# Gates projected with channels on the partitions, and probabilities divided by their sums

## The reference

```
h = RMSNorm(x);  P = h @ w_in[l]                 # (rows, 1024) @ (1024, columns of four branches)
A: sparse attention over the top 256 keys by an index score, 4 heads, one K/V head
B: attention with a forgetting term F[t] - F[s] on the logits, 4 heads, s <= t
C: attention in a band of 9 chunks of 64, learned bias on t - s, 4 heads
M: attention into 256 memory rows, 4 heads
parts = [o * silu(P[gate columns of the branch])  for the four outputs o]   # 256 columns each
x = x + concat(parts) @ w_out[l]
```

## Time and profile before

| what | value |
|---|---|
| median of 3 runs | 1713.21 us |
| lowest, highest | 1713.04, 1716.13 us |
| the profiled execution's own time | 1712.33 us |
| its span (first to last instruction) | 1710.5 us |
| TensorE busy | 1692.7 us, 99% |
| VectorE busy | 1005.7 us, 59% |
| ScalarE busy | 662.3 us, 39% |
| GpSimd busy | 239.7 us, 14% |
| granted TensorE clock, mean | 0.999 |

### The profile page before, as it was taken

The page is one execution under the profiler, slowest core; times in us unless marked ns, Lnnn a source line. Parts: engine busy times, 40 slices in busy tenths (PEclk is TensorE's granted clock), DMA queues, the critical chain, the costliest instruction groups (busy, mean ns, idle before and its releaser), DMA issues.

```text
span 1710.5 us, 30251 instructions
## 1 busy us (share of the span) xinstructions
PE 1692.7 (99%) x10866; PEld 1103.7 (65%) x10866; DVE 1005.7 (59%) x2707; ACT 662.3 (39%) x1599; POOL 239.7 (14%) x452
## 2 busy tenths in 40 slices
PE   9999999999999999999999999999999999999998
PEld 4466677767778755555444677767777886555553
DVE  3645888778878333333235378887888772333321
ACT  4532334333343345454124323343333433445531
POOL 1233321100010010002012433220000001000000
PEclk9999999999999999999999999999999999999999
DMA  8344322223132322114421533231231324221130
GB/s 285 94 143 126 127 94 87 97 78 106 41 134 94 103 79 97 40 47 115 129 94 51 166 104 127 94 137 44 81 109 38 132 97 121 69 90 37 46 108 37
DMA packets 60340, 166.64 MB, mean 97 GB/s; under 512 B 11345, under 2 KB 29745, under 8 KB 57889
## 3 DMA queue, kind: packets, MB, share of 16 engines
q1 hardware_dynamic: 43584, 125.88, 23.0%
q0 software_dynamic: 16608, 38.83, 6.9%
HBM read 137.03 MB, written 30.73 MB: 98 GB/s over the span
## 4 chain that ended last, share of the span: by engine, by line
PE 80%; DVE 14%; DMA 2%; issue 2%; ACT 1%; DVEq 1%; ACTq 0%; SPq 0%
PE psX L876 54%; DVE lower L1268 9%; PE psT L816 7%; PE psX L1052 6%; PE psS L985 6%; DVE work L1490 2%; PE psS L904 2%; DMA wring<-in_w 2%; PE psS L816 1%; PE psX L816 1%; PE psX L1027 1%; DVE gate L1322 0%; PE psS L954 0%; PE psS L924 0%; DVE sc L1434 0%
## 5 line engine op out<-in xcount | busy, mean ns | idle before, releaser
L876 PE MATMUL psX<-wring,hT 128*128 128x512 f32 (+2 forms) x2016 | 834.3, 557 | 6.4 <-ACT kv L1146 3.0
L876 PEld LDWEIGHTS psX<-wring,hT 128*128 128x128 f32 x2016 | 363.9, 190 | 327.5 <-issue 318.6
L1268 DVE TENSOR_SCALAR_CACHE_REDUCE lower<-sc,thr 128x640 uint8<-128x640 f32 (+5 forms) x462 | 407.3, 934 | 17.5 <-issue 9.5
L876 PE MATMUL psX<-hT,wring 128*128 128x128 f32 x2880 | 334.6, 275 | 0.9 <-ACT gate L1166 0.4
L876 PEld LDWEIGHTS psX<-hT,wring 128*128 128x128 f32 x2880 | 327.7, 192 | 3.6 <-issue 3.0
L1208 ACT ACTIVATE work<-work,stat 128x256 f32<-128x256 f32 (+7 forms) x288 | 200.0, 694 | 295.9 <-DVEq L1493 293.3
L1217 ACT COPY work<-psT 128x512 f32<-128x512 f32 (+2 forms) x352 | 156.7, 488 | 321.0 <-PE psT L816 319.7
L816 PEld LDWEIGHTS psT<-con,work 128*128 128x128 f32 x1080 | 121.4, 141 | 73.2 <-issue 66.5
L816 PE MATMUL psT<-con,work 128*128 128x128 f32 x1080 | 158.2, 278 | 0.0
L1490 DVE CUSTOM_DVE_ANT_0 work<-psS,bias 128x640 f32<-128x640 f32 (+7 forms) x120 | 86.2, 718 | 41.9 <-issue 20.5
L1490 DVE CUSTOM_DVE_ANT_0 work<-psS,sc 128x384 f32<-128x384 f32 (+5 forms) x48 | 42.8, 891 | 72.1 <-PE psT L816 70.0
(11 more groups left out here) (203 smaller groups left out, 1537.9 us busy)
## 6 DMA issues: line engine op xcount, KB each, us to landing
wring<-in_w SPq DMA_DIRECT2D x17, 2048.0 KB, 9.4
cache<-in_kB SPq DMA_DIRECT2D x16, 512.0 KB, 7.0
cache<-in_vB SPq DMA_DIRECT2D x16, 512.0 KB, 4.1
cache<-in_kC SPq DMA_DIRECT2D x16, 512.0 KB, 6.8
cache<-in_vC SPq DMA_DIRECT2D x16, 512.0 KB, 4.7
scratch_oscr<-gate POOLq DMA_DIRECT2D x54, 128.0 KB, 2.0
hT<-scratch_oscr SPq DMA_DIRECT2D x18, 384.0 KB, 3.6
kv<-in_x SPq DMA_DIRECT2D x9, 512.0 KB, 5.7
```

The costliest lines, as they stand in the source:

```text
L876: mm = pe.matmul(out, lhs, rhs, start=(kt == 0), stop=(kt == KT - 1))
L1268: v.tensor_scalar(lower[:, at:at + STRIP_L[t]], sc[:, o], thr[:, n:n + 1], 0.0, ALU.is_lt, ALU.add, accum_out=below[:, n:n + 1])
```

## The change

The gates' columns now come first in B2, C2 and A2, and two blocks of them are turned; M1 is turned whole. So the gate leaves the projection with its channels on the partitions, as the gating wants it, and V needs no transposes of it and ScalarE no copy (L1223). R is written with the two operands exchanged, so that its result comes out turned, and GT is gone.

A row's reciprocal can't be multiplied into a gate that has rows along the free axis. It is multiplied into the probabilities instead, before T: Z is split into Z 0 and the last Z. Z 0 takes the reciprocals of the even heads on VectorE, and ScalarE multiplies their exponentials (L1222 after); the other takes those of the odd heads, and VectorE multiplies them itself (L1499 after). T of a pack waits for its multiplications and not for its exponentials. Z 0 stands ahead of L 1, the last Z behind the second half of the selection's rounds, before the end of the unit. A pack's sums for samples are still divided where they were (L1513).

```diff
-TURNED = {"mm": 2, "B1": 4, "C1": 4, "M1": 2}
+TURNED = {"mm": 2, "B1": 4, "B2": 2, "C1": 4, "C2": 2, "M1": 4, "A2": 2}
@@ program_order
-        if prev:
-            emit("Z", prev)
         if prev and not fresh:
             emit("T", prev, 0)
...
             if pack and len(buffers(pack)) == 2:
+                emit("Z", pack, 0)
                 emit("L", pack, 1)
...
+    def weigh():
+        if pipe[0] and not weighed[0]:
+            emit("Z", pipe[0], buffers(pipe[0])[-1])
+            weighed[0] = True
...
     def settle():
         odd_heads()
+        weigh()
+        weighed[0] = False
...
         odd_heads()
         select(pace[0] / 2)
+        weigh()
         emit("P", c, t)
@@ TensorE, T
-                    pe.wait_ge(*probs.on((p, [i for i in range(heads(p)) if i % 2 == hp][-1])))
+                    if is_sample(p):
+                        pe.wait_ge(*probs.on((p, 0)))
+                    else:
+                        pe.wait_ge(*weighed[hp].on(p))
@@ TensorE, V
-                    pe.wait_ge(*scaled.on(p))
...
-                    for i in range(0, nh, 2):
-                        g = (h0 + i) // 2
-                        turn(o[:, W + i // 2 * P:W + (i // 2 + 1) * P], gates(br)[:, t, g * P:(g + 1) * P])
@@ TensorE, R
-                            mm = pe.matmul(X.ap(s)[32 * j:32 * j + 32, g * P:(g + 1) * P],
-                                           con[:, C_SELG + 32 * g:C_SELG + 32 * g + 32], om[:, j, :], start=True, stop=True)
+                            mm = pe.matmul(X.ap(s)[:, g * P + 32 * j:g * P + 32 * j + 32], om[:, j, :],
+                                           con[:, C_SELG + 32 * g:C_SELG + 32 * g + 32], start=True, stop=True)
@@ ScalarE, after a unit
+                        xg, rest = (x[:, W:2 * W], None) if c == "M1" else (x[:, 0:W], x[:, W:2 * W])
@@ ScalarE
-                elif k == "V" and not is_sample(s[1]):
-                    br, t, h0, nh = s[1]
-                    act.wait_ge(*X.fill(s).on(s))
-                    nc.scalar.copy(merged(br, t, h0 // 2, nh // 2),
-                                   X.ap(s)[:, W:W + nh * HD].rearrange("p (g c) -> p g c", g=nh // 2))
-                    act.drain().then_inc(g_turned.sem, 1)
+                elif k == "Z" and s[2] == 0 and not is_sample(s[1]):
+                    p = s[1]
+                    act.wait_ge(*inverted.on(p))
+                    for i in range(0, heads(p), 2):
+                        x = buf(0)[:, offset(p, i):offset(p, i) + blocks(p) * P]
+                        last = nc.scalar.mul(x, x, stats(p)[:, 2, i:i + 1])
+                    last.then_inc(weighed[0].sem, 1)
@@ VectorE, Z
-                    dve.wait_ge(*probs.on((p, n - 1)))
-                    v.reciprocal(stats(p)[:, 2, 0:n], stats(p)[:, 1, 0:n])
+                    dve.wait_ge(*probs.on((p, [i for i in range(n) if i % 2 == hp][-1])))
+                    last = v.reciprocal(stats(p)[:, 2, hp:n:2], stats(p)[:, 1, hp:n:2])
+                    if hp == 0 and not is_sample(p):
+                        last.then_inc(inverted.sem, 1)
                     dve.drain()
-                    if not is_sample(p):
-                        ga = gates(br)[:, t, h0 * HD:(h0 + n) * HD].rearrange("p (h d) -> p h d", h=n)
-                        v.tensor_tensor(ga, ga, stats(p)[:, 2, 0:n].unsqueeze(2).to_broadcast([P, n, HD]), ALU.mult)
-                        dve.drain()
-                    dve.drain().then_inc(scaled.sem, 1)
+                    if hp:
+                        for i in range(1, n, 2):
+                            x = buf(hp)[:, offset(p, i):offset(p, i) + blocks(p) * P]
+                            last = v.tensor_scalar(x, x, stats(p)[:, 2, i:i + 1], None, ALU.mult)
+                        last.then_inc(weighed[1].sem, 1)
@@ the weights' columns
-... "B2": join("b_v", "b_g") ... "C2": join("c_v", "c_g") ... "A2": join("a_q", "a_g")
+... "B2": join("b_g", "b_v") ... "C2": join("c_g", "c_v") ... "A2": join("a_g", "a_q")
```

More of the change, by code:

```diff
@@ L207, in settle @@
             emit("R", old[0])
-            gather.append(old[0])
     def project(c, t):
@@ L319, in program_order @@
         to_norm, normed = [], []
-        while queue or pipe != [None, None] or gather or outs or to_norm:
-            work = bool(queue) or pipe != [None, None] or bool(gather)
+        while queue or pipe != [None, None] or outs or to_norm:
+            work = bool(queue) or pipe != [None, None]
             if work:
@@ L331, in program_order @@
                     normed.append(t)
-            done = [s for s in o if s[0] == l and s[1][0] in ("V", "GT")]
-            ready = lambda t: (l, ("GT", "A")) in done if t == ST_ else (l, ("V", packs_of("A", t)[-1])) in done
+            done = [s for s in o if s[0] == l and s[1][0] in ("V", "R")]
+            ready = lambda t: (l, ("R", "A")) in done if t == ST_ else (l, ("V", packs_of("A", t)[-1])) in done
             if outs and ready(outs[0][1]):
@@ L650, in encoder @@
         pt_act = Signal(sem("probs_turned"), packs)
-        scaled = Signal(sem("gate_scaled"), packs)
-        g_turned = Signal(sem("gate_turned"), [p for p in packs if not is_sample(p[1])])
+        prompts = [p for p in packs if not is_sample(p[1])]
+        inverted = Signal(sem("sums_inverted"), prompts)
+        weighed = [Signal(sem(f"probs{hp}_weighed"), prompts) for hp in range(2)]
         om_ready = Signal(sem("own_heads_kept"), [p for p in packs if is_sample(p[1])])
         gated = Signal(sem("branch_gated"), [(l, s[1]) for l, s in order if s[0] == "R" or (s[0] == "V" and not is_sample(s[1]))])
-        gathered = Signal(sem("samples_turned"), events(["GT"], lambda s: s[1]))
         selected = Signal(sem("selected"), [(l, s[1][1]) for l, s in order if s[0] == "K" and s[1][0] == "mask"])
@@ L1067, in _ @@
                     turn(T.ap(s)[:, 0:P], om[:, 2, :]).then_inc(T.fill(s).sem, 1)
-                elif k == "GT":
-                    br = s[1]
-                    pe.wait_ge(*gated.on(br))
-                    pe.wait_ge(T.empty(s).sem, T.free(s))
-                    for b in range(2):
-                        mm = turn(T.ap(s)[:, b * P:(b + 1) * P], gates(br)[:, ST_, b * P:(b + 1) * P])
-                    mm.then_inc(T.fill(s).sem, 1)
         @block.scalar
@@ L1519, in _ @@
                     dve.wait_ge(*X.fill(s).on(s))
-                    dve.wait_ge(*g_turned.on(s[1]))
-                    o = merged(br, t, h0 // 2, nh // 2)
-                    v.tensor_tensor(o, X.ap(s)[:, 0:nh * HD].rearrange("p (g c) -> p g c", g=nh // 2), o, ALU.mult
+                    ga = gates(br)[:, t, h0 * HD:(h0 + nh) * HD].rearrange("p (g c) -> p g c", g=nh // 2)
+                    v.tensor_tensor(merged(br, t, h0 // 2, nh // 2),
+                                    X.ap(s)[:, 0:nh * HD].rearrange("p (g c) -> p g c", g=nh // 2), ga, ALU.mult
                                     ).then_inc(X.empty(s).sem, 1)
@@ L1526, in _ @@
                     dve.wait_ge(*X.fill(s).on(s))
-                    ga = gates(s[1])[:, ST_, :]
-                    v.tensor_tensor(ga, X.ap(s)[:, 0:W], ga, ALU.mult).then_inc(X.empty(s).sem, 1)
+                    two = lambda ap: ap.rearrange("p (g c) -> p g c", g=2)
+                    v.tensor_tensor(merged(s[1], ST_, 0, 2), two(X.ap(s)[:, 0:W]), two(gates(s[1])[:, ST_, :]), ALU.mult
+                                    ).then_inc(X.empty(s).sem, 1)
                     dve.drain().then_inc(gated.sem, 1)
@@ L1763, in _ @@
                     store(d["oscr"][t * P:(t + 1) * P, GCOL[br] - W:GCOL[br]], gate[:, t, :], o_stored[t].sem)
-                elif k == "GT" and s[1] != "A":
+                elif k == "R" and s[1] != "A":
                     br = s[1]
-                    pool.wait_ge(*gathered.on(br))
+                    pool.wait_ge(*gated.on(br))
                     store(d["oscr"][ST_ * P:, GCOL[br] - W:GCOL[br]], gate[:, ST_, :], o_stored[ST_].sem)
```

33 lines of the change are left out of this document (11 added, 22 removed).

## The result

The changed kernel takes 1739.12 us (median of 4 runs, 1737.78 to 1740.95) against 1713.12 for the kernel before (1712.73 to 1716.13): +26.0 us, a ratio of 1.0149 with a 95% interval of 1.0131 to 1.0166. The forecast was 1731 with a range of 1719 to 1740. The sign and the range hold, the range with 0.9 us to spare; the forecast's own narrower range, 1724 to 1737, does not. Nearly half of the time (11.8 us of the profiled 25.1) comes from a place that the sum had at nothing, and two terms of the sum were about twice too large. That these errors partly cancel is luck.

What follows compares the result with a forecast made beforehand. VectorE was taken to bound the selection stretches, TensorE the rest: 0.5 (TensorE) + 7.4 (B) + 8.9 (C) + 1.4 (end at 548.29) = +18.2 us on the profiled 1712.33, about 1731 as median, range 1719 to 1740.

Steps and rivals of the forecast that it cites:

- two terms of the sum: VectorE's added work in the selection stretches, over both layers: +7.4 us in B and +8.9 us in C.
- TensorE's sum: All TensorE changes: +10.8 turned blocks, -15.8 removed transposes, +9.6 R, together +4.6 us; outside the selection stretches +0.5.
- VectorE's term: Selection stretches: split reciprocals and odd heads' multiplications count one for one, +7.4 us in B and +8.9 in C.
- the extra 0.1: Selection stretches: 0.1 us added to each pack's VectorE cost, beside 0.6 for two reciprocals and the multiplications.
- 0.4 for the wait of the first pack of C: C stretch of each layer: Z1 waits for ScalarE's exponentials, now behind two multiplications, adding 0.4 us.
- T0 at the first pack of C: TensorE's T0 waits for Z0 and two multiplications, some 2.7 us later, inside a stretch VectorE sets anyway.
- The output stage: About 720 to 795 us, layer 0: no added cost forecast, the time from 640 to 840 us unchanged.
- the prediction's own sign of being wrong: Wrong if the stretches keep their length, or if TensorE waits for the weighing in stretches without selection.
- at nothing but at two places: ScalarE's even-head multiplications: free except at the exponentials of C,0 and the end of M, and T0 of (C,0).
- TensorE alone: Rival: only TensorE's work counts, VectorE's extra finds slack in the stretches; +4.6 us, 1718 us, chance 0.13.
- Dearer pieces: Rival: VectorE's pieces cost more or wait twice, 6 us a stretch; +26 us or more, 1740 us, chance 0.13.
- The second rival: VectorE is relieved, stretches shrink to TensorE's pace and give back its waits; +0.9 us, 1713 us, chance 0.06.

Runs made afterwards that it cites:

- doubled multiplications: Changed kernel with the odd heads' multiplication on VectorE done twice in branches B and C: 1763.74 us, ratio 1.0287.
- late Z: Changed kernel with the last Z behind the residual add and the norm's copy on VectorE, in the output stage only: 1728.93 us, ratio 1.0092.
- late Z and R in four: Changed kernel with the output stage's last Z behind the residual add, and R in four matmuls of 64 moving columns: 1721.50 us, ratio 1.0039.
- odd heads on GpSimd: Kernel with late Z and R in four, and the odd heads' multiplication moved from VectorE to GpSimd: 1721.75 us, ratio 1.0042.

## Why the prediction was right, and where it was wrong

**TensorE's sum** was right, +4.6 against the trace's +3.8, and in each price: +0.16 for a mixed unit, +0.12 for M1 (7.15 after), 0.11 for a transpose, 0.112 for R's record. The mixed unit is best seen at the first B2 unit: 7.24 after, where the same unit took 7.08. The trace agrees with the value that I took between 0.07 and 0.2, and the loads' side of it is in the trace too: R's loads of 128 columns take 192 ns recorded, those of 32 columns before 109. The exchange of R's operands costs 6 us of the 26, as R's operands put back show, against 4.8 in the forecast.

**VectorE's term** had the right mechanism and about twice the size: B and C were to bring 16.3 and brought 7.7, of which 1.7 is the clock in layer 1's C. VectorE's busy time in these four stretches rose by 9.2 us, where 4.05 for each was forecast. Three parts of its sum were too dear. (1) I took a multiplication's duration as its price, 2 x 0.29 for the first pack; the row at 360.27 has both in 0.48, since one starts before the other's recorded end. (2) A Z 0 costs 0.25 with its hand-over, not 0.30 (the counting row before it ends 0.52 us ahead of the logits at 358.65, 0.27 before), and the extra 0.1 was not there. (3) The old Z took 1.00 at this pack, where I used 0.90. Together the pieces of this pack take 0.90 us, 0.25 and 0.65, against 1.00 before, where the sum had +0.38. The 0.4 for the wait of the first pack of C did not come either: the reciprocal waits 0.61 us at 360.02 as the old one did. That the stretches have no slack left is shown by the doubled multiplications: 15.6 us more of VectorE in them, 14.9 us more of length.

**T0 at the first pack of C** was forecast to wait 2.7 us and did, 2.86, and in layer 0 it is mostly swallowed: the whole stretch is 1.0 longer. In layer 1 the granted clock falls to 0.83 behind it, 1.7 us that I had not.

**The output stage** is the step that failed, and the prediction's own sign of being wrong, TensorE waiting for the weighing in a stretch without selection, came true: 9.0 us of waits and 3.4 of lower clock behind them, where it had the time from 640 to 840 us unchanged. The prediction costed ScalarE's multiplications "at nothing but at two places", and counted VectorE's pieces outside the stretches as free because VectorE is busy there for a third of the time (68.51 of 200 us). It should have asked what stands behind the new wait in VectorE's queue. Busy shares can't answer that: in a window where VectorE idles 64% of the time, it held up TensorE three times by 3 us, since the piece that it idled on stood ahead of a copy that TensorE needed. The late Z gave 10.2 us back. Had the sum had this term beside its VectorE term it would have passed 1740; the two errors, 8.6 us too much in the stretches and 11.8 too little here, hide each other, and the measured time lies in the range by that luck.

**The clock** was in no term. Of the five waits of about 3 us (three in the output stage, two at C) three have a stretch of lower clock behind them, which cost 1.7 us each, 5.1 in all.

**The rivals.** TensorE alone (1718) is out. Dearer pieces (1740) has the time but not the reason: VectorE's pieces were cheaper than I had, not dearer. The second rival's gain is real but small, 1.8 us of idle time in the stretches, and seen only when the weighing is out.

## What to carry to other kernels

When a change adds a wait to an engine, list what stands behind it in that engine's queue and who waits for that; an engine that idles two thirds of a stage can still hold up the one that bounds it. Put an instruction that waits for another engine behind all that others are waiting for, and not close behind the instruction that starts the other engine's work. Dividing attention's probabilities costs work that grows with the keys (11.9 us here at best), dividing the outputs or the gate does not; turning the gates by the projection, with R in four matmuls, was worth 4.9 us, and it was lost because it forced the first.

## What the hardware did that I had not expected

- The granted clock fell behind single waits: after 3.13 us of waiting the window from 740 to 750 us has 0.83, and score matmuls took 3.30 in place of 1.77 to 1.99; the lower of the two levels, 1.2 GHz, for part of the window. Behind the wait of 2.86 us at 359 us in layer 0 it stayed at 1.00, and behind one of 2.23 us in the kernel with doubled multiplications a window has 0.66. The two waits at the first packs of C, 5.5 to 5.7 us together in each of these kernels, had it fall in layer 1 alone (the changed kernel), in layer 0 alone (late Z), in neither (late Z and R in four) and in both (odd heads on GpSimd). What decides between them stays open.
- A TENSOR_SCALAR of 640 columns takes 2.0 us on GpSimd, 0.55 on VectorE and, as an activation, 0.83 on ScalarE.
- One load of 128 columns serves a moving operand of two parts, 64 columns, in the time of one with 32: the records start about 0.11 us apart in both.
